# Layer norm in two token halves, statistics on token partitions, a GpSimd power, and the S5 tables spread anew over the first FFN

## The chip, the cores and the metric

The kernel runs on 1 core of one Trainium2 chip. The metric is device time in microseconds, the median of 3 runs. Engine names in the rows: PE is TensorE (PEld its weight loads), DVE is VectorE, ACT is ScalarE, POOL is GpSimd, SP is SyncE. A queue is written SPq or ACTq.

## The reference

Two hybrid decoder layers on 528 tokens (512 and 16 learned meta tokens), model width 1024, float32. Per layer there are three layer norms, after the first FFN, after the gated merge and after the second FFN:

```python
def layer_norm(x, g, b):
    mu = mean(x); var = mean(square(x - mu))
    return (x - mu) * rsqrt(var + LN_EPS) * g + b

x = layer_norm(ALPHA * x + 0.5 * swiglu(x, ...ffn1...), ln1_g, ln1_b)
proj = x @ w_in            # latents, short conv, S5 inputs, gates
y_a, y_b, y_c = attention, short conv, S5 state space model
x = layer_norm(ALPHA * x + (sum of sigmoid(g_i) * y_i) @ w_o, ln2_g, ln2_b)
x = layer_norm(ALPHA * x + 0.5 * swiglu(x, ...ffn2...), ln3_g, ln3_b)
```

`swiglu` is `(silu(x @ w_gate) * (x @ w_up)) @ w_down`, with an inner width of 2816, which is 22 tiles of 128.

## The kernel before

Activations are kept transposed: features on the 128 partitions, the 528 tokens along the free axis, so that x is 8 tiles of 128x528. Each float32 matrix product is made of three fast products in the fp32r format: every operand is split into a high part (`x_hi`, `w_hi`) and a rest (`x_lo`, `w_lo`), and `product` runs hi*hi, lo*hi and hi*lo. A product tile of 528 tokens fills two PSUM banks with 264 tokens each; `pair(k)` is banks 2k and 2k+1 of the 8, `two(x)` is x seen as 2x264. So a weight chunk of 1024 columns costs 8 tiles x 3 products x 2 token halves = 48 matmuls, one of 768 columns 36.

Weights come as 236 chunks for each layer. A chunk `c` goes through four engines. SP loads it into one of two `w_raw` slots once GpSimd has finished with the chunk two before; ACT rounds it to `w_hi` (`round_ahead`, three chunks ahead, as soon as PE is through with the chunk that held the slot); GpSimd makes `w_lo = w_raw - w_hi` (`split`); PE multiplies and counts `chunk_done`. Each engine runs its own list of instructions in order, and the engines meet in semaphores only.

An FFN runs in three parts (`PARTS`, of 8, 8 and 6 inner tiles). In a part, each inner tile needs two chunks (gate and up); ACT applies Silu, and DVE multiplies (L1185) and splits the result (L1186, L1187). Then eight down chunks follow (8 tiles x nf), whose products DVE adds to the residual `z` ("ln_in" in the rows) with one instruction each. While the first FFN runs, DVE also computes the tables of the S5 branch: eight `in_step`s beside the inner tiles of part 0, eight `turn_step`s beside its down chunks, `out_step`s beside part 1.

A norm (`layer_norm` on DVE, `layer_norm_middle` and `layer_norm_end` on PE, `square` and `layer_norm_end` on ACT) works like this. After four of the last eight chunks PE sums the features of z0 to z2 over partitions with a matrix of ones (a 128x128 stationary operand of ones gives the sum in all 128 partitions, L467), and DVE takes this provisional mean away from all tiles. DVE adds up tiles and squares as the other chunks end. PE then sums both over partitions (L467), DVE computes mean and variance for 128x528, ACT takes the root, DVE the reciprocal (L1164). After that each tile passes DVE (scale, L1167), ACT (gain and bias in place, then `x_hi`), and DVE (`x_lo`, L1170), which counts `x_ready`. The next stage begins with `first_products` (L458), which runs three chunks side by side, tile by tile, as `x_ready` counts up. Before the change, the products of all last chunks and of `first_products` write both token halves of a tile.

## Time and profile before

| what | value |
|---|---|
| median of 3 runs | 2853.81 us (2849.2 to 2854.4) |
| the profiled execution, its own time | 2849.89 us |
| its span, first to last instruction | 2848.1 us |
| PE busy | 2680.8 us, 94% |
| DVE / ACT / POOL busy | 1403.8 / 845.6 / 1052.7 us |
| granted TensorE clock, mean | 0.976 of full |

Busy is the share of the span in which an engine has an instruction in work. The profiled execution lies 3.9 us below the median.

### The profile page before, as it was taken

To read this page: it belongs to the slowest core of one execution; us is meant where nothing else is said; L and a number is where in the kernel's file an instruction comes from. 1 tells how busy PE (TensorE), PEld (TensorE's weight loads), DVE (VectorE), ACT (ScalarE), POOL (GpSimd) and SP (SyncE) were. 2 spreads that over 40 slices of the span, in tenths; PEclk is the share of its full clock that TensorE was granted. 3 is DMA by queue.
4 is the path that set the end of the run, shared out by engine and by line. 5 is a ranking of instruction groups with operands and counts; after the bars stand their busy time and mean duration, and the time that the engine had idled before them with its cause. 6 is when DMAs were issued, how large, how long until landed. Compare 5 with 4: busy or idle time off the path is not lost.

```text
span 2848.1 us, 56824 instructions
## 1 busy us (share of the span) xinstructions
PE 2680.8 (94%) x22244; PEld 2601.3 (91%) x22244; DVE 1403.8 (49%) x2020; ACT 845.6 (30%) x1236; POOL 1052.7 (37%) x477
## 2 busy tenths in 40 slices
PE   7999988999999989999789999799999998999996
PEld 7999988988889989999789999799888998999995
DVE  6955154954443652121688641648545337522127
ACT  3222223225522242222242212232345222422123
POOL 3444433322244434444234444233122443344431
PEclk9999999999999999999899999999999999999998
DMA  4323323212223323332223332232122332233322
GB/s 144 96 82 93 89 78 83 71 33 59 55 79 92 97 67 89 89 92 85 69 87 89 89 89 85 71 90 68 40 50 67 78 92 82 82 89 89 89 81 75
DMA packets 458208, 229.30 MB, mean 81 GB/s; under 512 B 38112, under 2 KB 455136, under 8 KB 458048
## 3 DMA queue, kind: packets, MB, share of 16 engines
q1 hardware_dynamic: 452864, 219.98, 27.8%
q10 hardware_dynamic: 5184, 7.14, 0.9%
q8 instruction: 106, 1.74, 0.2%
q14 instruction: 54, 0.44, 0.0%
HBM read 222.83 MB, written 2.10 MB: 79 GB/s over the span
## 4 chain that ended last, share of the span: by engine, by line
issue 51%; PE 25%; POOL 21%; DVE 2%; POOLq 1%; ACT 0%; DMA 0%; SPq 0%; DVEq 0%; ACTq 0%
PE ps L442 21%; POOL w_lo L393 21%; PE ps L458 1%; PE ps L742 1%; PE ps L704 1%; PE ps L721 0%; DVE ln_in L1133 0%; PE ps L467 0%; POOLq L392 0%; PE ps L708 0%; DVE stat L1164 0%; DVE stat L1148 0%; DVE ln_in L1117 0%; POOLq L398 0%; DVE stat L1134 0%
## 5 line engine op out<-in xcount | busy, mean ns | idle before, releaser
L393 POOL TENSOR_TENSOR w_lo<-w_raw,w_hi 128x1024 fp32r<-128x1024 f32 (+3 forms) x472 | 1050.0, 2230 | 1748.0 <-ACT w_hi L830 1747.9
L830 ACT ACTIVATE w_hi<-w_raw 128x1024 fp32r<-128x1024 f32 (+3 forms) x475 | 453.8, 959 | 851.6 <-PE ps L442 724.2
L442 PE MATMUL ps<-x_hi,w_hi 128*128 128x264 f32 x4000 | 543.1, 288 | 20.6 <-ACT w_hi L830 8.1
L442 PEld LDWEIGHTS ps<-x_hi,w_hi 128*128 128x128 f32 x4000 | 507.8, 190 | 32.6 <-issue 23.5
L442 PE MATMUL ps<-x_lo,w_hi 128*128 128x264 f32 x4000 | 528.4, 284 | 0.0
L442 PE MATMUL ps<-x_hi,w_lo 128*128 128x264 f32 x4000 | 526.5, 284 | 0.0
L442 PEld LDWEIGHTS ps<-x_lo,w_hi 128*128 128x128 f32 x4000 | 502.9, 189 | 0.0
L442 PEld LDWEIGHTS ps<-x_hi,w_lo 128*128 128x128 f32 x4000 | 501.0, 188 | 0.0
L1185 DVE TENSOR_TENSOR hid_rest<-hid_rest,ps 128x528 f32<-128x528 f32 x88 | 61.9, 704 | 548.5 <-PE ps L442 524.2
L442 PE MATMUL ps<-hid_hi,w_hi 128*128 128x264 f32 x1408 | 195.8, 290 | 15.5 <-DVE ln_in L1117 14.6
L442 PEld LDWEIGHTS ps<-hid_hi,w_hi 128*128 128x128 f32 x1408 | 181.6, 192 | 18.6 <-DVE ln_in L1117 16.1
L442 PE MATMUL ps<-hid_lo,w_hi 128*128 128x264 f32 x1408 | 190.3, 285 | 0.0
L442 PE MATMUL ps<-hid_hi,w_lo 128*128 128x264 f32 x1408 | 188.9, 284 | 0.0
L442 PEld LDWEIGHTS ps<-hid_lo,w_hi 128*128 128x128 f32 x1408 | 179.6, 190 | 0.0
L442 PEld LDWEIGHTS ps<-hid_hi,w_lo 128*128 128x128 f32 x1408 | 178.0, 189 | 0.0
L1198 DVE SCALAR_TENSOR_TENSOR ln_in<-ps,ln_in 128x528 f32<-128x528 f32 x64 | 45.3, 707 | 255.6 <-PE ps L442 254.4
L1187 DVE TENSOR_TENSOR hid_lo<-hid_rest,hid_hi 128x528 fp32r<-128x528 f32 x88 | 152.8, 1736 | 3.1
L830 ACT ACTIVATE hid_rest<-ps 128x528 f32 x88 | 53.8, 611 | 331.7 <-PE ps L442 331.6
L458 PE MATMUL ps<-x_hi,w_hi 128*128 128x264 f32 x288 | 64.6, 308 | 64.5 <-DVE x_lo L1170 45.1
L1522 DVE SCALAR_TENSOR_TENSOR stat<-stat,ps 128x528 f32<-128x528 f32 x32 | 22.5, 705 | 184.5 <-PE ps L442 184.5
L458 PEld LDWEIGHTS ps<-x_hi,w_hi 128*128 128x128 f32 x288 | 49.6, 209 | 67.2 <-DVE x_lo L1170 47.2
L830 ACT ACT_TABLE_LOAD x53 | 68.0, 1283 | 94.4 <-PE ps L442 59.6
(272 smaller groups left out, 2928.3 us busy)
## 6 DMA issues: line engine op xcount, KB each, us to landing
w_raw<-in_ffn_w_gate SPq DMA_DIRECT2D x91, 512.0 KB, 3.8
w_raw<-in_w_in SPq DMA_DIRECT2D x90, 512.0 KB, 3.9
w_raw<-in_ffn_w_up SPq DMA_DIRECT2D x88, 512.0 KB, 3.8
w_raw<-in_ffn_w_down SPq DMA_DIRECT2D x64, 512.0 KB, 3.9
w_raw<-in_ffn_w_down SPq DMA_DIRECT2D x32, 384.0 KB, 3.3
w_raw<-in_w_o SPq DMA_DIRECT2D x16, 512.0 KB, 3.8
w_raw<-in_conv_w_out SPq DMA_DIRECT2D x16, 256.0 KB, 2.8
w_raw<-in_s_w_out SPq DMA_DIRECT2D x16, 256.0 KB, 3.2
```

The costliest lines, as they stand in the source:

```text
L393: pool.tensor_tensor(w_lo[:, s, 0:n], w_raw[:, c % RAW, 0:n], w_hi[:, s, 0:n].bitcast(f32), ALU.subtract).then_inc(w_split, 1)
L442: ins = nc.tensor.matmul(out[0:m, h], w[:, s, cols], x[:, k0 + k, h * HALF:(h + 1) * HALF], start=first and k == 0 and n == 0, stop=last a ...
L458: ins = nc.tensor.matmul(out[:, h], w[:, (c + j) % SLOTS, k * P:(k + 1) * P], x[:, k, h * HALF:(h + 1) * HALF], start=k == 0 and n == 0, s ...
L704: ins = nc.tensor.matmul(ps[:, j % 2, 0:q0 + P], qT[0:QKD, b, q0:q0 + nq], kT[0:QKD, b, 0:q0 + P], start=True, stop=True)
L742: ins = nc.tensor.matmul(ps[64 * b:64 * b + 64, 4 + 2 * b + half, q0 - half * HALF:HALF], vb[0:nk, b, k, :], PT[0:nk, k, q0:(half + 1) * H ...
L830: return nc.scalar.activation(out, in_, f, **kw)
L1185: st.done(tt(two(glf[:, f]), two(glf[:, f]), pair(2 * (f % 2) + 1), MUL))
L1187: tt(gl[:, f], glf[:, f], ghf[:, f], SUB).then_inc(hid_done, 1)
L1198: ins = stt(two(z[:, d]), pair(d % 2), 0.5 / ALPHA, two(z[:, d]), MUL, ADD)
L1522: ins = stt(two(stat[:, 2]), two(stat[:, n % 2]), 1.0, pair(2 * (n % 2) + 1), ADD, MUL)
```

## The change

Tokens 0 to 263 and 264 to 527 become two halves that pass through a norm one after the other. The last four down (or w_o) chunks are multiplied for the first half, all four, and then for the second half, each 128x264 result in a bank of its own (`HALF_BANK`, `last_tiles`). DVE takes each half tile out of PSUM, takes the provisional mean away and adds it to the sums (`take_half`); ACT squares it. The provisional mean is that of z0 and z1, and stays in PSUM. The sums over features are now made with the tokens as output partitions: the stationary operand is 88 tokens of the sums, the moving operand one column of ones, so that the 264 tokens of a half give 88 partitions x 3 columns (`layer_norm_sums`). DVE computes mean and variance on these 88x3 elements with four instructions, GpSimd raises the variance to the power -0.5 (`root`, `norm`), and PE spreads the mean and the root back over 128 partitions and 264 columns with a matmul against the identity (`layer_norm_wide`); DVE reads both from PSUM (`tail`). ACT no longer uses Sqrt in a norm, DVE no reciprocal there.

The next stage's first four chunks are multiplied for the first half of the tokens and then for the second: two chunks tile by tile, the sums of the second half, the third chunk, the spreading of the second half, the fourth chunk, and then all four for the second half. GpSimd's splits of these four chunks stand between its two powers; ACT's roundings of them stand between its norm tiles. Three of DVE's four `take_half`s of the second half stand in the first half's `tail`, behind tiles 0, 3 and 5.

`PARTS` becomes 6, 8 and 8 inner tiles, so that the last down chunks have 48 matmuls instead of 36. In the first FFN the S5 tables move: `s5_parameters` behind the first inner tile, `in_step`s 0 to 4 in part 0 and 5 to 7 in part 1, `turn_step`s 0 to 5 beside part 0's down chunks and 6 and 7 in part 1, `out_step`s 1 to 3 in part 1 and 4 to 7 in part 2; PE's transposes of them (`turn_inputs`) go from part 0's down chunks to part 1's. z is no longer rebuilt from `x_hi` and `x_lo` in the FFNs (it still holds x); before the w_o norm it is rebuilt in the merge loop. ACT's S5 parameter functions come after the Silu of the first inner tile, and the output leaves in 16 transfers instead of 8.

```diff
-PARTS = [(0, 8), (8, 8), (16, 6)]
+PARTS = [(0, 6), (6, 8), (14, 8)]
 PART_AT = [sum(2 * nf + KD for _, nf in PARTS[:n]) for n in range(len(PARTS))]
...
+HALF_BANK = {4: 0, 5: 2, 6: 1, 7: 3}
...
+            for h, t0 in enumerate((N_META, HALF)):
+                t1 = (h + 1) * HALF
+                for k in range(KD):
+                    sp.wait_ge(ln_out, (3 * DEPTH - 1) * 2 * KD + h * KD + k + 1)
+                    sp.dma_start(t["out"][k * P:(k + 1) * P, t0 - N_META:t1 - N_META], z[:, k, t0:t1]).then_inc(out_written, 16)
+            sp.wait_ge(out_written, 32 * KD)
...
+            def root(l, which, h):
+                pool.wait_ge(ln_var, (l * 3 + which) * 2 + (h + 1))
+                pool.tensor_tensor(tok_root[0:TOK, h], tok_root[0:TOK, h],
+                                   minus_half[0:TOK, :].to_broadcast([TOK, TB]), ALU.pow).then_inc(ln_root, 1)
+            def norm(l, which, c0):
+                root(l, which, 0)
+                for n in range(SLOTS):
+                    split(l, c0 + n)
+                root(l, which, 1)
...
+            def first_products(l, c, x0, n):
+                for h in range(2):
+                    for j in range(2):
+                        pe.wait_ge(z_half[1], n * 4 + (4 + 2 * h + j + 1))
+                    by_tiles(l, [pair(0), pair(1)], c, xh, xl, x_ready[h], x0, halves=(h,))
+                    if h == 0:
+                        layer_norm_sums(n, 1)
+                    for j in (2, 3):
+                        rounded(l, c + j)
+                        ins = product(pair(j), c + j, 0, xh, xl, KD, True, True, split=(l, c + j), halves=(h,))
+                        if h == 1:
+                            ins.then_inc(chunk_done, 1)
+                        elif j == 2:
+                            layer_norm_wide(n, 1)
...
+            def layer_norm_first(l, which):
+                n = l * 3 + which
+                pe.wait_ge(ln_sums, n * 3 + 2)
                 sum_over_features(stat[:, 1], pair(2)).then_inc(ln_stat, 1)
...
+            def layer_norm_sums(n, h):
+                pe.wait_ge(ln_sums, n * 3 + (h + 3))
+                for src, bank in ((stat[:, 1], 4 + h), (stat[:, 2], 6 + h)):
+                    for j in range(TB):
+                        t0 = h * HALF + j * TOK
+                        ins = nc.tensor.matmul(ps[0:TOK, bank, SUM_AT + j:SUM_AT + j + 1], src[:, t0:t0 + TOK],
+                                               ones[:, 0:1], start=True, stop=True)
+                    ins.then_inc(ln_stat, 1)
+            def layer_norm_wide(n, h):
+                pe.wait_ge(const_in, 16 * 5)
+                for ready, src, bank in ((ln_mean, tok_mean, 4 + h), (ln_root, tok_root, 6 + h)):
+                    pe.wait_ge(ready, n * 2 + (h + 1))
+                    for j in range(TB):
+                        ins = nc.tensor.matmul(ps[:, bank, j * TOK:(j + 1) * TOK],
+                                               src[0:TOK, h, j:j + 1].to_broadcast([TOK, P]), ident[0:TOK, 0:TOK],
+                                               start=True, stop=True)
+                    ins.then_inc(ln_wide, 1)
+            def last_tiles(l, which, c, hi, lo, nk):
                 n = l * 3 + which
...
+                t0 = takes_at(l, which, (len(PARTS) - 1) * (which != 1))
+                for h in range(2):
+                    for d in range(WHOLE, KD):
+                        if h == 0:
+                            rounded(l, c + d)
+                            pe.wait_ge(z_taken, t0 + (min(d, 5) + 1))
+                        else:
+                            pe.wait_ge(z_half[0], n * 4 + (d - 3))
+                        bank = HALF_BANK[d]
+                        s = (c + d) % SLOTS
+                        for p, (w, x) in enumerate(((w_hi, hi), (w_hi, lo), (w_lo, hi))):
+                            if p == 2 and h == 0:
+                                split_ready(l, c + d)
+                            for k in range(nk):
+                                ins = nc.tensor.matmul(ps[:, bank, 0:HALF], w[:, s, k * P:(k + 1) * P],
+                                                       x[:, k, HALVES[h]], start=p == 0 and k == 0,
+                                                       stop=p == 2 and k == nk - 1)
+                        ins.then_inc(half_done if h == 0 else chunk_done, 1)
+                        if h == 1 and d == WHOLE:
+                            layer_norm_sums(n, 0)
+                        if h == 1 and d == WHOLE + 1:
+                            layer_norm_wide(n, 0)
...
+                act.wait_ge(ln_dev, n * 12 + (k + 1 if h is None else 1 + k + 4 * h))
+                dst = stat[:, 2] if k == 0 else stat[:, 3 + k % 2]
+                ACTV(dst[:, cols], z[:, k, cols], ACT.Square).then_inc(ln_square, 1)
+            def norm_tile(l, which, k, h):
+                n = (l * 3 + which) * 2 + h
+                col = PC_LN + which * 16 + k
+                act.wait_ge(ln_scaled, n * KD + (k + 1))
+                ACTV(z[:, k, HALVES[h]], z[:, k, HALVES[h]], ACT.Identity, scale=par[:, col:col + 1],
+                     bias=par[:, col + 8:col + 9]).then_inc(ln_out, 1)
+                act.wait_ge(ln_out, n * KD + (k + 1))
+                ACTV(xh[:, k, HALVES[h]], z[:, k, HALVES[h]]).then_inc(ln_hi, 1)
+            def layer_norm(l, which, bd):
+                for d in range(WHOLE):
+                    round_ahead(l, bd + d)
+                for k in range(3):
+                    square(l, which, k)
+                round_ahead(l, bd + WHOLE)
+                square(l, which, 3)
+                for k in range(4, KD):
+                    square(l, which, k, 0)
+                square(l, which, 4, 1)
+                round_ahead(l, bd + 5)
                 for k in range(KD):
...
+                    norm_tile(l, which, k, 0)
+                    if k in (1, 4, 6):
+                        square(l, which, {1: 5, 4: 6, 6: 7}[k], 1)
+                        round_ahead(l, bd + {1: 6, 4: 7, 6: 8}[k])
+                for k in range(KD):
+                    norm_tile(l, which, k, 1)
...
+                def take_half(k, h):
+                    if h == 0:
+                        dve.wait_ge(half_done, n * 4 + (k - 3))
+                    else:
+                        dve.wait_ge(chunk_done, done_at(l, bd + k))
+                    cols = HALVES[h]
+                    ins = stt(z[:, k, cols], ps[:, HALF_BANK[k], 0:HALF], scale, z[:, k, cols], MUL, ADD)
+                    follow(ins, z_half[h], n * 4 + (k - 3) + 4 * h)
+                    follow(tt(z[:, k, cols], z[:, k, cols], ps[:, 6 + h, 0:HALF], SUB), ln_dev, n * 12 + (1 + k + 4 * h))
+                    st.done(tt(S[:, cols], S[:, cols], z[:, k, cols], ADD))
+                def add_square(k, cols=every, square=None):
+                    dve.wait_ge(ln_square, n * 12 + square)
+                    return tt(Q[:, cols], Q[:, cols], stat[:, 3 + k % 2, cols], ADD)
                 take(0)
                 take(1)
...
+                tt(S, z[:, 0], z[:, 1], ADD).then_inc(ln_sums, 1)
                 take(2)
...
+                dve.wait_ge(ln_stat, n * 5 + 3)
+                st.done(ts(pair(3), pair(2), 1.0 / (2 * P), None, MUL))
+                st.done(stt(two(S), pair(3), -2.0, two(S), MUL, ADD))
+                for k in range(3):
+                    tt(two(z[:, k]), two(z[:, k]), pair(3), SUB).then_inc(ln_dev, 1)
+                dve.wait_ge(ln_dev, n * 12 + 3)
+                st.done(tt(S, S, z[:, 2], ADD))
+                st.done(add_square(1, square=2))
                 take(3)
...
+                follow(tt(two(z[:, 3]), two(z[:, 3]), pair(3), SUB), ln_dev, n * 12 + 4)
+                st.done(tt(S, S, z[:, 3], ADD))
+                st.done(add_square(2, square=3))
+                for k in range(WHOLE, KD):
+                    if k == WHOLE:
+                        st.done(add_square(3, square=4))
+                    else:
+                        st.done(add_square(k - 1, HALVES[0], k))
+                    take_half(k, 0)
+                add_square(KD - 1, HALVES[0], KD).then_inc(ln_sums, 1)
+                take_half(WHOLE, 1)
+                def tail(h):
+                    cols = HALVES[h]
+                    mean, root = ps[:, 4 + h, 0:HALF], ps[:, 6 + h, 0:HALF]
+                    sums, squares = (ps[0:TOK, b + h, SUM_AT:SUM_AT + TB] for b in (4, 6))
+                    m_, v_, t_ = (v[0:TOK, h] for v in (tok_mean, tok_root, tok_tmp))
+                    dve.wait_ge(ln_stat, n * 5 + (4 + 2 * h))
+                    follow(ts(m_, sums, 1.0 / D_MODEL, None, MUL), ln_mean, n * 2 + (h + 1))
+                    st.done(tt(t_, m_, m_, MUL))
+                    dve.wait_ge(ln_stat, n * 5 + (5 + 2 * h))
+                    st.done(stt(v_, squares, 1.0 / D_MODEL, t_, MUL, SUB))
+                    ts(v_, v_, LN_EPS / ALPHA ** 2, None, ADD).then_inc(ln_var, 1)
+                    dve.wait_ge(ln_wide, n * 4 + (2 * h + 3))
+                    dev = lambda k: tt(z[:, k, cols], z[:, k, cols], mean, SUB)
+                    dev(0)
+                    st.done(dev(1))
+                    dve.wait_ge(ln_wide, n * 4 + (2 * h + 4))
+                    m = n * 2 + h
+                    for k in range(KD + 1):
+                        if k < KD:
+                            tt(z[:, k, cols], z[:, k, cols], root, MUL).then_inc(ln_scaled, 1)
+                        if k + 2 < KD:
+                            st.done(dev(k + 2))
+                        if k:
+                            dve.wait_ge(ln_hi, m * KD + k)
+                            tt(xl[:, k - 1, cols], z[:, k - 1, cols], xhf[:, k - 1, cols], SUB).then_inc(x_ready[h], 1)
+                        if h == 0 and k in (1, 4, 6):
+                            j = {1: 5, 4: 6, 6: 7}[k]
+                            st.done(add_square(j - 1, HALVES[1], j + 4))
+                            take_half(j, 1)
+                        if h == 0 and k == 7:
+                            add_square(KD - 1, HALVES[1], 12).then_inc(ln_sums, 1)
+                tail(0)
+                tail(1)
...
+            def tables_beside(l, part, f, st):
+                if part == 0 and f == 0:
+                    s5_parameters(l, st)
+                    dve.wait_ge(b_in, l * 32 + 32)
+                if part == 0 and f > 0:
+                    in_step(l, f - 1, st)
+                if part == 1:
+                    if f < 3:
+                        in_step(l, f + 5, st)
+                    elif f == 3:
+                        turn_step(l, 6, st)
+                    elif f == 4:
+                        turn_step(l, 7, st)
+                        cmul(st, [bS[:, 0], bS[:, 1]], each(s5cf[:, 0], 32), each(s5cf[:, 1], 32), by_pair(bS[:, 0]),
+                             by_pair(bS[:, 1]), 32)
+                    else:
+                        out_step(l, f - 4, st)
+                if part == 2 and f < 4:
+                    out_step(l, f + 4, st)
```

## Rows read from the trace of the kernel before

**Rows 1.** Waits of PE: who waited for whom (us in all, times, longest)
```profile
PE ps L458 <- DVE x_lo L1170: 45.1, 5, 9.1
PE ps L442 <- DVE ln_in L1198: 3.2, 4, 1.2
```

**Rows 2.** Windows, PE alone, one per norm: length, busy (matmuls), clock
```profile
395.50:458.00 62.50, 46.09 (x311) 0.84 0.20 51
968.70:1030.20 61.50, 48.81 (x359) 0.92 0.18 52
1381.60:1451.90 70.30, 46.65 (x310) 0.83 0.19 59
1810.00:1871.30 61.30, 43.45 (x310) 0.92 0.20 51
2381.90:2444.10 62.20, 49.83 (x359) 0.89 0.16 48
2795.50:2848.10 52.60, 25.07 (x166) 0.75 0.21 70
```

**Rows 3.** Timeline of PE, first norm: start, length, instructions merged, [idle before]
```profile
395.53 1.05 PE L467 MATMUL ps<-stat,ones 128*128 128x264 f32 x4
...
408.39 3.01 PE L442 MATMUL ps<-hid_hi,w_hi 128*128 128x264 f32 x12 [3.08 <-DVE ln_in L1117]
...
457.97 2.10 PE L442 MATMUL ps<-x_hi,w_hi 128*128 128x264 f32 x16
459.91 2.10 PE L442 MATMUL ps<-x_lo,w_hi 128*128 128x264 f32 x16
```

**Rows 4.** Timeline of PE where layer 1 begins
```profile
1451.90 3.89 PE L442 MATMUL ps<-x_hi,w_hi 128*128 128x264 f32 x16 [7.46 <-POOL w_lo L393]
```

**Rows 5.** Timelines of DVE and ACT, and one group by shape: sizes
```profile
48.58 0.41 DVE L1257 TENSOR_TENSOR s_tmp<-s_coef,s_b_own 128x256 f32<-128x256 f32 x1
...
437.91 0.81 ACT L830 ACTIVATE ln_in<-ln_in,par 128x528 f32<-128x528 f32 x1
438.75 0.64 ACT L830 ACTIVATE x_hi<-ln_in 128x528 fp32r<-128x528 f32 x1
...
L830 ACT ACTIVATE s_u<-ps 128x264 f32<-128x264 f32 x16 | 5.3, 390 | 9.4 <-PE ps L458 9.4
```

**Rows 6.** Timeline of PE in the heads: small plain float32 matmuls
```profile
656.52 0.42 PE L721 MATMUL ps<-ident,probs 16*128 16x16 f32 x4
```

**Rows 7.** Timeline of DVE, first norm: reciprocal, two tiles of the new x
```profile
432.28 3.44 DVE L1164 RECIPROCAL stat<-stat 128x528 f32<-128x528 f32 x1
...
438.04 0.71 DVE L1170 TENSOR_TENSOR x_lo<-ln_in,x_hi 128x528 fp32r<-128x528 f32 x1 [0.21 <-ACT x_hi L830]
...
440.02 0.70 DVE L1170 TENSOR_TENSOR x_lo<-ln_in,x_hi 128x528 fp32r<-128x528 f32 x1
```

**Rows 8.** Groups of POOL by shape, the two smallest
```profile
L393 POOL TENSOR_TENSOR w_lo<-w_raw,w_hi 128x256 fp32r<-128x256 f32 x16 | 13.6, 851 | 34.0 <-ACT w_hi L830 34.0
L1623 POOL MEMSET const-float32-0.0<- 128x1 f32 x1 | 0.1, 100 | 0.3 <-issue 0.3
```

**Rows 9.** Lines L1185 and L1187 (ns min/median/max), and a split beside DVE
```profile
L1185 DVE TENSOR_TENSOR hid_rest<-hid_rest,ps x88: 690/704/705, 41.2 to 2778.2; 128x528 f32<-128x528 f32 x88
L1187 DVE TENSOR_TENSOR hid_lo<-hid_rest,hid_hi x88: 707/1470/2896, 42.4 to 2779.4; 128x528 fp32r<-128x528 f32 x88
...
416.40 2.53 POOL L393 TENSOR_TENSOR w_lo<-w_raw,w_hi 128x1024 fp32r<-128x1024 f32 x1 [3.85 <-ACT w_hi L830]
416.59 2.90 DVE L1148 TENSOR_TENSOR stat<-stat 128x528 f32<-128x528 f32 x1
```

**Rows 10.** Timeline at the kernel's end
```profile
2844.94 0.71 DVE L1170 TENSOR_TENSOR x_lo<-ln_in,x_hi 128x528 fp32r<-128x528 f32 x1 [0.68 <-ACT x_hi L830]
```

**Rows 11.** Timeline of PE at the kernel's start
```profile
18.31 0.81 PE L458 MATMUL ps<-x_hi,w_hi 128*128 128x264 f32 x2 [1.43 <-POOL w_lo L393]
...
40.29 2.10 PE L442 MATMUL ps<-x_hi,w_hi 128*128 128x264 f32 x16
```

289 lines of the change are left out of this document (114 added, 175 removed).

## Prediction

> **What bounds the kernel now.** I read the page first: PE is busy for 94% of the span, every other engine half of it or less, and inside the FFNs PE waits for almost nothing. So the question is where its missing time lies. The waits of PE say it: its largest wait is for `x_lo`, five times 9 us [rows 1]. These are the norms. The reader is to see the same hole six times in the windows [rows 2]: each window runs from the provisional sum (after the fourth of the last eight chunks) to the product behind the first three chunks of the next stage; the sixth ends with the kernel.
>
> The price of a hole is its length less the matmuls in it at full pace. Sixteen matmuls take 1.94 us, 0.121 each (the last two rows of [rows 3]). An FFN norm holds 4 x 36 + 3 x 48 = 288, or 34.8 us; a w_o norm 336, or 40.6 us. The losses: 62.5 - 34.8 = 27.7; 61.5 - 40.6 = 20.9; 70.3 - 34.8 = 35.5; 61.3 - 34.8 = 26.5; 62.2 - 40.6 = 21.6. Behind the third comes a run of 16 matmuls in 3.9 instead of 1.9 us [rows 4], 1.9 more: together 134 us. The sixth holds 144 matmuls (17.4 us) in 52.6 us: 35.2 lost. In the timeline of the first norm the reader sees what a loss is made of: PE waits 3 us for DVE among the last chunks (408.4), again before the sums [rows 3], then 9 us for the root, the reciprocal and the first tile [rows 1].
>
> **A norm after the change, step by step.** Half a tile of a down chunk is 24 matmuls, 2.9 us. T = 0 is where PE starts the first half of chunk 4 of the last eight. I lay out each engine's list in order.
>
> Sizes: a DVE operation on 128x256 takes 0.41 us, and on 264 columns I take 0.43. ACT takes 0.39 for a 128x264 copy; gain and bias on 528 columns is 0.17 longer than `x_hi` (0.81, 0.64), so 0.62 and 0.43 for the half [rows 5]. These are estimates from the rows. One `take_half` with its `add_square` is four DVE operations that wait for each other: 1.8 us.
>
> First halves, T = 0 to 11.6. DVE needs 1.8 us of each 2.9. It starts at 5.7, behind the third tile, three sums and a split that holds one of them, has caught up when the fourth half arrives, and its sums are ready at 13.7. PE sums at 14.5, after chunk 4's second half. Small plain float32 matmuls are two instructions each; four instructions of 16x16 stand in 0.42 us [rows 6], so 0.1 apiece, so that a set of six matmuls (12 instructions) is 1.2 us. Four sets per norm: 4.8 us, and 0.9 for the provisional sum, one matmul set of the kind that takes 1.05 us with its end [rows 3]. DVE's four 88x3 operations end at 16.7.
>
> GpSimd's power has no row. From below it costs 0.1 (its MEMSET on 128x1); from above I take the 0.85 of 128x256 subtracted, times the 5 by which DVE's reciprocal (3.44 us [rows 7]) exceeds its plain operation of that size (0.70), about 4. I take 1.0, since 3 columns are nearest to the MEMSET's one [rows 8]. PE spreads mean and root after chunk 5, at 18.6, so the first power is hidden up to 1.9 us; the second is on the path. At 4 us each it would cost 5 us per norm, 30 in all: that is an end of the range.
>
> `tail` for the first half begins at 20.4. Before, a tile passed every 1.98 us (438.04 to 440.02) [rows 7]. A half tile is three DVE operations in 1.15 us and two on ACT in 1.1. Three tiles carry a `take_half`, 1.8 us, and on ACT a square and a rounding, 1.5 us. And the splits now run beside the tiles: before, the roundings they wait for stood behind ACT's last tile. An operation with one operand in PSUM is never held (690 to 705 ns over 88); one with both in SBUF is held until the split ends (707 to 2896 ns, one stands beside its split) [rows 9]. The subtractions and products of `tail` read PSUM and pass, `x_lo` and the sums don't. Laid out in order, `x_lo` is ready at 22.5, 25.5, 28.3, 29.6, 32.6, 35.4, 37.9 and 41.2: three of the four splits hold an `x_lo` for about 1.5 us.
>
> PE has ended the last chunk at 26.0. The two first chunks need 5.8 us, but are fed until 41.2 and end at 41.95: 10.1 us lost. Then the sums (43.2), the third chunk (46.1), the spreading with the power just in time (47.7), the fourth chunk (50.6). The second half's tiles come from 50.1 every 1.25 us, with no splits among them, so PE ends them at 59.6: 3.2 us lost. Then 5.8 us of work, to 65.4. Work of 384 matmuls is 46.5. Loss: 65.4 - 46.5 + 0.9 = 19.8.
>
> The clock: after a wait of 3.1 us the first 12 matmuls took 3.0 instead of 1.6 us [rows 3]. Feeding in bursts should bring that once or twice. I add 2.0: **21.8 per norm**, five times 109.
>
> TensorE's small matmuls are where a page would price otherwise. The Trainium skill, TensorE: Matmul & The Clock Gate, section "Wait — 56ns, not 53.3ns?", has starts no closer than about 25 ns however few the columns. By it the 48 instructions of a norm would take 1.2 us (estimate from that page), and the change would be worth some 20 us more; the rows of the heads, four times slower, decide here, since each instruction also loads weights.
>
> The sum. Five norms: 109 - 134 = -25. The last norm: the same list, the second sums already at 38.4, the statistics done at 43.8, last tile out of ACT at 53, last transfer 2.5 us behind (2845.65 to 2848.1) [rows 10]: 55.4 + 0.9 - 23.2 = 33.1 lost, against 35.2: -2. The start: two chunks instead of three must be split before PE runs through, so from 18.3 [rows 11]; with 23.2 us of work, 2.4 for an empty sum and spreading and 1.4 of slow clock the fourth chunk ends at 45.3, against 40.3 + 5.8 = 46.1: -1.
>
> The S5 tables. With eight in_steps beside eight inner tiles of 11.6 us (96 matmuls) PE's wait for what DVE takes between parts is 3.2 us over all four FFNs [rows 1]. The new places hold no more work per tile, and z's rebuilding (0.7 per tile) is gone. Tighter are the down chunks of part 0, 36 matmuls or 4.35 us instead of 5.8: the largest step there, six operations on 128x256, is 2.5 us, with the take of 0.7 and a split in between 5.7. The two bank pairs take the overrun up. All at nothing, hidden behind PE's products; with the cover gone it would be 1 or 2 us. But ACT's parameter functions, with their table loads, now stand between two roundings of a running stage: round chunk 4 at 4.9 after the halves end, the functions wait for DVE behind the first inner tile, and chunk 5 is ready about 1 us after PE wants it: +1 per layer, +2. The stall of 7.5 us that the same functions cause at the second layer's start [rows 4] is in the third window above, so it is not counted again. Longer last chunks (`PARTS`) cost nothing, they move matmuls from part 0.
>
> -25 - 2 - 1 + 2 = -26. From the profiled execution's own 2849.9 us that gives 2824; the runs' median lies 3.9 above it, so I predict **2827**.
>
> **Rivals.**
> *Hidden after all.* If PSUM reads and the split times fall luckily (no `x_lo` held, 4.5 us; one clock fall less, 1), a norm loses 16.3: five 82, total -53, 2800. For it: the powers and sums of the first half lie behind products. Against: in the first `tail` DVE alone has 14.6 us of work (8 x 1.15 + 3 x 1.8), where PE has 11.6.
> *The splits take it all.* GpSimd's four splits of 2.5 us could each hold DVE for their whole length, 10 us instead of 4.5, so 5.5 more per norm: +27, 2855, no change. The row shows the full hold of 2.2 us [rows 9]. The Trainium skill, SBUF — State Buffer, section "Who interferes with whom", has it as a rule: the port is locked for a whole instruction, and whoever issued first keeps it. By that rule four splits under a chain of DVE operations are a risk; the trace agrees.
> *Slower: the step doesn't halve.* The chain DVE, ACT, ACT, DVE with its semaphores may set the pace of a tile, so that a half tile takes near the 1.98 us of a whole one. Then the first `tail` is 7 x 0.8 = 5.8 longer and the second as much: 11.6 per norm, +58, 2885. It decides from 1.15 up to 1.15 + 5.2 / 14 = 1.5 us per half tile; above that the change loses. For it: fixed costs don't shrink, and there are twice as many hand-overs. Against: DVE's halves take 0.41 of 0.70, and the software order has two tiles in flight. A power of 4 us goes the same way, to 2855.
> *The clock stays low.* Bursts of 0.7 us each 2.5 us could keep TensorE at 1.2 GHz through all of the next four chunks. Against: at 408.4 it was back at full pace behind 12 matmuls [rows 3], and each of the new chunks has 24 in a row. Three falls of 1.4 to 1.8 us instead of one: 3 us more per norm, 2842. The Trainium skill, TensorE: Matmul & The Clock Gate, section "HAM oscillation — how this bites in real kernels", warns of just such work between waits.
>
> **How the numbers follow.** Forecast 0.50, between 2808 and 2845; hidden after all 0.22; splits take it all 0.10; slower 0.13; clock 0.05. The range leaves out the luckiest tenth and the slowest tenth: 2785 to 2862. A difference under 0.2% (5.7 us) this measurement can't tell from none. Faster: nearly all of the first two and the clock's, 0.76; same 0.09; slower 0.15.
>
> **What would show it.** In each norm: `x_lo` of the first half every 1.2 us with gaps where `take_half` stands, each of 1.8; PE waiting about 10 us in pieces before L458's successor, then some 3 us in the second half; DVE operations with two SBUF operands at up to 2.9 us beside splits, those from PSUM at 0.43; 12 small matmul instructions in 1.2 us; the power near 1 us; no long wait before chunk 5 of an FFN; the last tile's `x_hi` 53 us after T. Wrong would be: a power of several us, a half tile slower than 1.5 us, or PE fed so early that the first halves end at 32.

## The result, and the profile after

The changed kernel takes 2819.0 us (median of 4 runs, 2817.1 to 2822.2), the kernel before 2852.4 beside it: a ratio of 0.9885, 95% interval 0.9868 to 0.9902. The forecast was 2827. The profiled execution has a span of 2816.6 us against 2848.1, so 31.5 less, where the sum said 26.

First the waits of PE, all those of 1.2 us in sum or more but the ones inside the mixers, as the view groups them (total, times, longest). They answer to [rows 1].

```profile
PE ps L489 <- DVE x_lo L1289: 34.8, 41, 2.2
PE ps L489 <- POOL w_lo L408: 22.4, 6, 12.6
PE ps L528 <- DVE stat L1238: 12.1, 1, 12.1
PE ps L473 <- ACT w_hi L915: 7.0, 3, 3.8
...
PE ps L473 <- DVE hid_lo L1310: 2.9, 1, 2.9
...
PE ps L473 <- DVE ln_in L1317: 1.2, 2, 0.7
```

One wait of 9 us per norm for the first `x_lo` has become eight or so short ones. Then the windows of PE, one per norm, as in [rows 2] (length, busy and matmuls, granted clock, DMA). They begin at the provisional sum, which now stands a chunk earlier, and end with the fourth chunk of the next stage, one later than before: 432 matmuls, 52.2 us at full pace.

```profile
386.39:459.45 73.06, 65.16 (x486) 0.91 0.20 51
957.91:1031.82 73.91, 65.79 (x486) 0.91 0.18 53
1362.59:1435.66 73.07, 64.41 (x486) 0.93 0.22 63
1779.22:1852.20 72.98, 65.24 (x486) 0.91 0.20 52
2350.06:2424.21 74.15, 65.65 (x487) 0.91 0.18 53
2754.97:2816.60 61.63, 37.51 (x294) 0.80 0.25 76
```

The losses are 20.9, 21.7, 20.9, 20.8 and 22.0, together 106 us; 109 was forecast, and 134 stood before (with 1.9 behind the third window; 1.8 stand there now, and N3 in the table below has both). The last loses 32.6 (forecast 33.1). The first norm on PE's timeline, T = 0 at 393.10; it can be laid beside the forecast's list:

```profile
407.64 1.03 PE L528 MATMUL ps<-ones,stat 128*88 128x1 f32 x12
...
411.53 0.80 PE L538 MATMUL ps<-ident,token_mean 88*128 88x88 f32 x6
...
425.50 0.39 PE L489 MATMUL ps<-x_hi,w_hi 128*128 128x264 f32 x1 [1.89 <-DVE x_lo L1289]
...
428.01 0.59 PE L489 MATMUL ps<-x_hi,w_hi 128*128 128x264 f32 x1 [1.46 <-DVE x_lo L1289]
...
434.99 1.82 PE L528 MATMUL ps<-ones,stat 128*88 128x1 f32 x12
...
441.16 0.80 PE L538 MATMUL ps<-ident,token_mean 88*128 88x88 f32 x6
```

Sums at T = 14.5 (forecast 14.5), spread at 18.4 (18.6), the first halves' tiles done at 41.9 (41.95), the whole at 66.4 (65.4). The same twelve small instructions took 1.03 us in the first of these rows and 1.82 in the fifth, because the granted clock had fallen in between, while PE worked in bursts of 0.7 us between waits of 1 to 2 us. It was back for the second half (windows of PE, the clock is the last but two):

```profile
393.10:426.20 33.10, 29.67 (x247) 1.00 0.21 54
426.20:440.00 13.80, 10.22 (x48) 0.51 0.28 77
440.00:459.45 19.45, 18.55 (x143) 1.00 0.02 5
```

GpSimd's new group by shape, beside the smallest split's (busy and mean ns, idle before):

```profile
L408 POOL TENSOR_TENSOR w_lo<-w_raw,w_hi 128x256 fp32r<-128x256 f32 x16 | 13.6, 848 | 34.4 <-ACT w_hi L915 34.4
L424 POOL TENSOR_TENSOR token_root<-token_root,minus_half 88x3 f32<-88x3 f32 x12 | 10.2, 847 | 102.1 <-DVE token_root L1275 102.1
```

And the timelines of VectorE and GpSimd in the first norm:

```profile
425.01 0.43 DVE L1289 TENSOR_TENSOR x_lo<-ln_in,x_hi 128x264 fp32r<-128x264 f32 x1
...
426.01 1.95 DVE L1289 TENSOR_TENSOR x_lo<-ln_in,x_hi 128x264 fp32r<-128x264 f32 x1 [0.23 <-ACT x_hi L915]
...
425.10 2.57 POOL L408 TENSOR_TENSOR w_lo<-w_raw,w_hi 128x1024 fp32r<-128x1024 f32 x1 [4.37 <-ACT w_hi L915]
```

The power takes 0.85 us, and a split from 425.10 to 427.67 holds an `x_lo` that needs 0.43 until 427.96. So inside a norm nearly every row stands where it was forecast. The stretches outside don't. At the start of the first FFNs PE now waits for ScalarE:

```profile
66.86 3.01 PE L473 MATMUL ps<-x_hi,w_hi 128*128 128x264 f32 x16 [3.80 <-ACT w_hi L915]
...
1437.60 2.19 PE L473 MATMUL ps<-x_hi,w_hi 128*128 128x264 f32 x16 [1.77 <-ACT w_hi L915]
...
1445.08 2.17 PE L473 MATMUL ps<-x_hi,w_hi 128*128 128x264 f32 x16 [1.42 <-ACT w_hi L915]
```

while the second FFN has no wait left at all. In layer 1 these are the fifth and sixth chunks, whose roundings stand around the parameter functions. In layer 0 it is the eighth, and the rounding that it waits for had itself waited for a load:

```profile
65.69 1.06 ACT L915 ACTIVATE w_hi<-w_raw 128x1024 fp32r<-128x1024 f32 x1 [1.71 <-DMA w_raw<-in_ffn_w_gate]
```

A chunk is loaded into one of two slots when an earlier split has ended, so a rounding held up by the parameter functions (it stands at 47.43, behind them) makes a split late and with it the next load. That is read off the timelines; that the order is the cause, e7 tests. And before, the loss behind `w_o`, where the last tiles had 48 matmuls already, was 21, what it is now; only the norms behind an FFN gained. The following table is the frame for the experiments. Each number is what PE lost in a stretch of the profiled execution: its length less its matmuls at 0.1208 us each (16 in 1.933). N1 to N6 are the norms in order (N2 and N5 behind `w_o`; N3 up to the fifth chunk of layer 1, with the waits ahead of it); A1, A2 the first FFNs of the layers between the norms' windows, B1, B2 the second.

| kernel | N1 | N2 | N3 | N4 | N5 | N6 | A1 | B1 | A2 | B2 | span |
|---|---|---|---|---|---|---|---|---|---|---|---|
| before | 27.7 | 20.9 | 37.5 | 26.5 | 21.6 | 35.2 | 7.2 | 3.4 | 8.2 | 3.4 | 2848.1 |
| after | 20.9 | 21.7 | 22.8 | 20.8 | 22.0 | 32.6 | 10.3 | 0.2 | 11.0 | 0.2 | 2816.6 |
| e1 after, boundary wait back | 20.8 | 21.8 | 23.1 | 20.8 | 21.8 | 32.6 | 12.9 | 3.4 | 14.3 | 3.4 | 2825.6 |
| e2 before, boundary wait moved | 27.6 | 19.7 | 36.0 | 27.8 | 19.7 | 34.4 | 4.2 | 0.1 | 5.1 | 0.2 | 2827.2 |
| e3 before, parts 8, 6, 8 | 19.9 | 21.6 | 32.0 | 22.6 | 21.6 | 30.2 | 8.3 | 3.4 | 8.4 | 3.4 | 2825.9 |
| e4 after, parts 8, 8, 6 | 27.8 | 21.9 | 28.2 | 27.6 | 21.8 | 37.9 | 9.3 | 0.1 | 9.3 | 0.1 | 2837.6 |
| e5 before, both edits | 21.2 | 21.5 | 29.3 | 21.4 | 21.5 | 30.2 | 6.1 | 0.2 | 6.2 | 0.2 | 2813.8 |
| e6 e5, fourth chunk first | 19.9 | 21.0 | 22.1 | 21.4 | 21.5 | 30.2 | 5.3 | 0.2 | 15.0 | 0.2 | 2809.1 |
| e7 after, parameters later | 21.6 | 22.0 | 21.0 | 22.0 | 21.7 | 32.6 | 5.0 | 0.2 | 10.4 | 0.2 | 2810.3 |
| e8 after, spreads earlier | 21.1 | 21.1 | 22.1 | 21.1 | 20.7 | 32.6 | 10.1 | 0.2 | 12.3 | 0.2 | 2816.5 |
| e9 e6, parameters later | 19.9 | 21.4 | 20.0 | 21.2 | 21.5 | 30.2 | 15.6 | 0.2 | 13.9 | 0.2 | 2817.3 |
| e10 after, narrow splits | 13.8 | 16.6 | 15.8 | 16.6 | 18.0 | 28.9 | 11.3 | 0.2 | 10.8 | 0.2 | 2783.0 |
| e11 after, power thrice | 22.6 | 22.2 | 24.4 | 22.1 | 22.0 | 34.8 | 10.1 | 0.2 | 13.9 | 0.2 | 2830.5 |
| e12 e5, narrow splits | 16.2 | 15.4 | 22.7 | 15.8 | 16.6 | 30.1 | 5.3 | 0.2 | 7.6 | 0.2 | 2788.0 |

The start and the mixers make up the rest. The mixers' code is the same in all, and what their stretch in the second layer lost by the same count still varied from 123.5 to 129.2 us (e10 and e9 against e12), so a single span says nothing about less than some 5 us. Single norms are steadier: N2, which has the same code in before, e2, e3, e5, e6 and e9, lost 19.7 to 21.6. The ratios of the timed runs, each to the kernel before on its own chip, stand with each experiment.

### The profile page after: what moved, and what is told of

It reads as the page before. It is cut to its first block, busy times and chain, and to the rows that moved or that the text cites. A ratio compares the mean times of both kernels' runs of the same rounds, so it can differ in the third digit from the quotient of the medians.

```text
span 2816.6 us, 58024 instructions
## 1 busy us (share of the span) xinstructions
PE 2699.4 (96%) x22460; PEld 2619.6 (93%) x22460; DVE 1371.3 (49%) x2257; ACT 844.3 (30%) x1333; POOL 1069.1 (38%) x492
## 4 chain that ended last, share of the span: by engine, by line
issue 50%; PE 26%; POOL 22%; DVE 1%; POOLq 1%; ACT 1%; DMA 0%; SPq 0%; DVEq 0%; ACTq 0%
POOL w_lo L408 22%; PE ps L473 21%; PE ps L560 1%; PE ps L824 1%; PE ps L786 1%; PE ps L489 1%; PE ps L803 0%; DVE ln_in L1277 0%; DMA w_raw<-in_ffn_w_gate 0%; POOLq L407 0%; PE ps L790 0%; DVE ln_in L1284 0%; ACT w_hi L915 0%; PE ps L538 0%; DVE x_lo L1289 0%
## 5 line engine op out<-in xcount | busy, mean ns | idle before, releaser
L915 ACT ACTIVATE w_hi<-w_raw 128x1024 fp32r<-128x1024 f32 (+2 forms) x476 | 457.2, 964 | 844.4 <-PE ps L473 711.6
L473 PE MATMUL ps<-x_hi,w_hi 128*128 128x264 f32 x4096 | 561.7, 289 | 12.6 <-ACT w_hi L915 7.0
L915 ACT ACTIVATE hid_rest<-ps 128x528 f32 (+1 forms) x88 | 53.8, 611 | 366.3 <-PE ps L473 351.8
L473 PE MATMUL ps<-hid_hi,w_hi 128*128 128x264 f32 x1152 | 157.9, 286 | 1.2 <-DVE ln_in L1317 1.2
L473 PE MATMUL ps<-hid_hi,w_lo 128*128 128x264 f32 x1152 | 155.1, 284 | 0.0
L473 PE MATMUL ps<-hid_lo,w_hi 128*128 128x264 f32 x1152 | 155.0, 283 | 0.0
L473 PEld LDWEIGHTS ps<-hid_hi,w_hi 128*128 128x128 f32 x1152 | 146.0, 188 | 2.6 <-DVE ln_in L1317 1.6
L473 PEld LDWEIGHTS ps<-hid_hi,w_lo 128*128 128x128 f32 x1152 | 145.7, 188 | 0.0
L473 PEld LDWEIGHTS ps<-hid_lo,w_hi 128*128 128x128 f32 x1152 | 145.6, 188 | 0.0
L489 PE MATMUL ps<-x_hi,w_hi 128*128 128x264 f32 x192 | 66.3, 346 | 57.2 <-DVE x_lo L1289 34.8
L1661 DVE SCALAR_TENSOR_TENSOR stat<-stat,ps 128x528 f32<-128x528 f32 x32 | 22.6, 705 | 176.0 <-PE ps L473 176.0
L915 ACT ACTIVATE ln_in<-ln_in,par 128x264 f32<-128x264 f32 x96 | 57.6, 600 | 99.1 <-DVE ln_in L1284 98.9
```

Of the source, the lines that this page charges most:

```text
L473: ins = nc.tensor.matmul(out[0:m, h], w[:, s, cols], x[:, k0 + k, HALVES[h]], start=first and k == 0 and n == 0, stop=last and k == n_tile ...
L489: ins = nc.tensor.matmul(out[:, h], w[:, (c + j) % SLOTS, k * P:(k + 1) * P], x[:, k, HALVES[h]], start=k == 0 and n == 0, stop=k == KD - ...
L915: return nc.scalar.activation(out, in_, f, **kw)
L1661: ins = stt(two(stat[:, 2]), two(stat[:, n % 2]), 1.0, pair(2 * (n % 2) + 1), ADD, MUL)
```

## The experiments

**e1 and e2: one wait at the part boundaries.** The diff moves a line that the forecast passed over. Before, PE waited at the start of each FFN part for VectorE's take of the last down tile (`t0 + 2`). Now it waits there for the one before it, and for the last only ahead of the first up chunk, whose banks it frees. e1 undoes this in the changed kernel, e2 does it in the kernel before.

```diff
# e1, in the changed kernel
-                        pe.wait_ge(z_taken, t0 + 1)
+                        pe.wait_ge(z_taken, t0 + 2)
# e2, in the kernel before
-                    pe.wait_ge(z_taken, t0 + 2)
+                    pe.wait_ge(z_taken, t0 + (2 if part == 0 else 1))
...
                             rounded(l, c + 1, i * 4)
+                            pe.wait_ge(z_taken, t0 + 2)
```

> The changed kernel with one line as it was before: TensorE waits at the start of the second and third part of each FFN for VectorE's take of the last down tile, not of the one before it. Theory A (that take is late at each of the eight part boundaries; before, six waits of 1.35 us sum to 8.1 though the view puts them down to w_hi, and after none is there in the second FFN): 9 to 10 us slower than the changed kernel, 2828 to 2829, ratio to the kernel before 0.9915, with one wait of about 1.35 us at each boundary. Rival B (those waits are really for ScalarE's rounding, cured by the longer lead elsewhere): the same as the changed kernel, 2819.

> The kernel before with that one wait moved alone: at a part boundary TensorE waits for the take of the last but one down tile, and for the last one's only ahead of the first up chunk. Theory A: 8 to 10 us faster than before, 2843 (ratio 0.997), the six waits for w_hi of 8.1 us in the chain of TensorE's waits gone. Rival B: no change, 2852.

e1: 2831.2 us, ratio 0.9938 (0.9924 to 0.9951), against 0.9885 without the edit. e2: 2834.5 us, ratio 0.9945 (0.9932 to 0.9958), some 16 us faster than before. Theory A holds, and its price was too low: 3.0 to 3.3 us per FFN in e2 (A and B columns), 12.6 in all, as it takes 12.3 in e1. (The norms, the mixers and the start account for the rest of e2's span, 4.2, 3.2 and 0.9 us less; the edit doesn't touch them.) The view had put six of the eight waits down to the wrong engine. The boundary on PE's timeline in e1, then ScalarE and VectorE at that time, then the changed kernel's PE and ScalarE at the same boundary:

```profile
2512.90 1.83 PE L473 MATMUL ps<-x_hi,w_hi 128*128 128x264 f32 x13 [1.34 <-ACT w_hi L915]
...
2511.74 1.06 ACT L915 ACTIVATE w_hi<-w_raw 128x1024 fp32r<-128x1024 f32 x1 [3.30 <-PE ps L473]
...
2511.59 0.71 DVE L1317 SCALAR_TENSOR_TENSOR ln_in<-ps,ln_in 128x528 f32<-128x528 f32 x1 [3.64 <-PE ps L473]
```

```profile
2505.60 2.09 PE L473 MATMUL ps<-x_hi,w_hi 128*128 128x264 f32 x16
...
2505.95 1.06 ACT L915 ACTIVATE w_hi<-w_raw 128x1024 fp32r<-128x1024 f32 x1 [3.30 <-PE ps L473]
```

In e1 a rounding ends 0.1 us before PE starts, so it looks like the releaser. In the changed kernel PE starts 0.35 us before that same rounding begins: PE never needed it. The take ends at 2512.30; why PE needs 0.6 us more (its loop's set-up behind the wait would be one reason) was not tried.

**e3 and e4: the length of the last tiles.** `PARTS` moves two inner tiles from the first part to the last, so the tiles ahead of an FFN's norm have 48 matmuls, not 36. The forecast had that cost nothing and gain nothing. e3 does it alone, e4 undoes it (in both, table steps follow so that none is lost).

```diff
# e3, in the kernel before
-PARTS = [(0, 8), (8, 8), (16, 6)]
+PARTS = [(0, 8), (8, 6), (14, 8)]
# e4, in the changed kernel
-PARTS = [(0, 6), (6, 8), (14, 8)]
+PARTS = [(0, 8), (8, 8), (16, 6)]
```

> The kernel before with the FFN parts cut 8, 6, 8 in place of 8, 8, 6, so that the last down tiles are of 48 matmuls, not 36 (the tables follow). The matmuls are as many. Theory P (the norms behind an FFN lost 27 us and those behind w_o 21 only because their last tiles were shorter; both lose 21 after the change): 6 us less at each of three norms and 3 at the end, about 20 us faster, 2832. Rival H (it is the two halves that gain, the tiles' length does nothing): 2852. Between them the share of each can be read.

> The changed kernel with the FFN parts cut 8, 8, 6 as before: halves, statistics on tokens and power kept, last tiles of 36 matmuls. Theory P: the norms behind an FFN lose 6 us more again, 2837 to 2840. Rival H: 2819 to 2822.

e3: 2828.6 us, ratio 0.9923 (0.9908 to 0.9937), 22 us faster than before. e4: 2840.8 us, ratio 0.9967 (0.9955 to 0.9980), 23 us slower than the changed kernel by the ratios. Theory P holds both ways: N1, N4 and N6 go from 27.7, 26.5 and 35.2 to 19.9, 22.6 and 30.2 in e3, and from 20.9, 20.8 and 32.6 to 27.8, 27.6 and 37.9 in e4. So at N1 and N4 the halves with tiles of 36 lose what whole tiles of 36 lost before, and at N6 2.7 more. What the tile length does is on PE's timeline, first norm, of e5 (below), to be laid beside [rows 3] and beside this row of before, the wait for the sums:

```profile
423.27 3.89 PE L467 MATMUL ps<-stat,ones 128*128 128x264 f32 x8 [3.90 <-DVE stat L1148]
```

The rows of e5:

```profile
402.00 2.20 PE L442 MATMUL ps<-hid_hi,w_hi 128*128 128x264 f32 x16 [0.84 <-DVE ln_in L1118]
...
408.37 2.20 PE L442 MATMUL ps<-hid_hi,w_hi 128*128 128x264 f32 x16 [0.31 <-DVE ln_in L1118]
...
416.90 2.05 PE L467 MATMUL ps<-stat,ones 128*128 128x264 f32 x8 [2.46 <-DVE stat L1149]
...
429.83 0.81 PE L458 MATMUL ps<-x_hi,w_hi 128*128 128x264 f32 x2 [9.10 <-DVE x_lo L1171]
```

VectorE's rounds from one take to the next are as long in both kernels, 8.4, 6.4 and 7.1 us before and 8.3, 6.4 and 7.1 in e5. They outlast PE's tile of 4.35 us by far, its tile of 5.8 us by less. The 3.08 us ahead of 408.39 in [rows 3] are 0.84 here, and the wait for the sums 2.46 (3.90 before). The clock is part of the price: behind the longer waits the first twelve matmuls took 3.0 us and the eight of the sums 3.89, against 2.05 for these eight in e5. The 9.1 us for the first `x_lo` are untouched, and yet the loss is 21.

**e5 and e6: the kernel before with both edits, and with ScalarE's order too.** e5 is e2 and e3 together: whole-tile norms, no halves, no power. e6 adds this:

```diff
# e6, on top of e5; the first two f's are taken out of ScalarE's loop
                 st = Steps(act, act_step, l, ACT_STEPS)
+                round_ahead(l, B_FFN1)
                 act.wait_ge(x_ready, l * 24 + 8)
```

> The kernel before with the boundary wait moved (as in the run of it alone, which gave 3.2 us at each of four FFNs) and the parts cut 8, 6, 8 (which gave 8 us at the first norm, 4 and 2 at the third and fourth, 5 at the end); whole-tile layer norms, statistics and square root as before, no power on GpSimd. Theory P (the changed kernel's gain is these two, and the halves add nothing): 2848 - 13 - 19 to 21 = 2814 to 2817, ratio 0.987 to 0.988, so no slower than the changed kernel. Rival H (the gains overlap, and the halves carry the rest): 2825 or more.

> The run before this one, and ScalarE rounds the fourth chunk of a layer ahead of the wait for x_ready, its five DMA issues and the parameter functions, which are now behind it. Theory: the wait of 7.5 us for that chunk's w_lo at the second layer's start goes, with the slow clock behind it, 8 to 10 us less than the kernel with both edits, 2805 to 2808, faster than the changed kernel by 11 to 14. Rival: the x_lo that the chunk's products then wait for takes it over, and less than 3 us are gained.

e5: 2817.2 us, ratio 0.9893 (0.9878 to 0.9908). That is the changed kernel's 0.9885 within both intervals: **two edits of a few lines give the whole gain, and the halves give none of it.** In the table e5's norms lose 145.1 us in sum and the changed kernel's 140.8; all of the difference and more is N3 (29.3 against 22.8), the wait of 7.7 us for the fourth chunk's `w_lo`, and that is ScalarE's order again. The four norms with neither that wait nor the kernel's end in them, N1, N2, N4 and N5, lose 85.6 us in e5 and 85.4 in the changed kernel; at N6 the halves lose 2.4 more.

Why the halves gain nothing can be read off the first norm. In e5 PE waits 12.7 us (0.84, 0.31, 2.46 and 9.10), and its sums over features take 4.5. In the changed kernel no wait is longer than 2 us, but the two stretches that are fed tile by tile lose 10.5 and 2.4 us, 12.9 together, and the small sums and spreads take 5.8. The rest is mostly the lower clock: 3.0 us in e5's products behind its long wait, 1.5 in the changed kernel's third chunk. The wait was cut into pieces, not shortened.

e6: 2815.9 us, ratio 0.9888 (0.9872 to 0.9904). N3 gives its 7.2 us, as expected, but A2 takes 8.8 back: the rival's outcome, though with another row than it named. PE's one long wait in that FFN:

```profile
1443.17 3.86 PE L442 MATMUL ps<-x_hi,w_hi 128*128 128x264 f32 x16 [6.97 <-DVE hid_lo L1198]
```

The reading was that VectorE stands at its parameters ahead of the first inner tile, so that a PE that comes earlier only waits later.

**e7 and e9: the parameters later.** e7 puts ScalarE's five parameter DMA issues and its parameter functions behind the second Silu, and moves VectorE's table steps one inner tile on. e9 does it on top of e6.

```diff
# e7, ScalarE of the changed kernel
                 gate(0, 0, 0, ahead=False)
+                gate(0, 0, 1)
                 if w == 0:
+                    parameter_loads(l)
                     act.wait_ge(s5p_in, l * 16 + 16)
...
-                gate(0, 0, 1)
# e7, VectorE
-                if part == 0 and f == 0:
+                if part == 0 and f == 1:
                     s5_parameters(l, st)
# e9, VectorE's in-steps j by inner tile f
+                            for j in {2: (0,), 3: (1,), 4: (2,), 5: (3,), 6: (4, 5), 7: (6, 7)}.get(f, ()):
```

> The changed kernel with ScalarE's parameter DMA issues and parameter functions behind the second Silu of a layer's first FFN, and VectorE's table steps one f later. Theory: TensorE's waits of 3.8 + 3.2 us for w_hi and 2.9 us for hid_lo at the start of the first FFNs (losses there 10.3 and 11.0 us against 4.2 and 5.1 with the boundary wait alone moved) shrink by 8 to 10 us in all, 2809 to 2811. Rival: the parameters come late for VectorE, which then holds up hid_lo of the next f for as long, 2819 or more.

> The kernel before with the boundary wait moved, parts 8, 6, 8, ScalarE's fourth chunk first (the three of the last such run), and now the parameter DMA issues and functions behind the second Silu as well, VectorE's parameters behind the second f and its in-steps behind f = 2 to 7. The last such run saved 7 us at the third norm and gave 9 back in the second layer's first FFN (a wait of 7.0 us for hid_lo). Theory: that wait was VectorE standing at its parameters ahead of the first f; both gains hold, the first FFN of the second layer loses 5 to 6 us and the third norm 22, 2800 to 2806, ratio 0.984 to 0.986. Rival: the longer run of parameters between two f holds hid_lo up elsewhere, no faster than 2813.

e7: 2812.7 us, ratio 0.9876 (0.9860 to 0.9893), the fastest kernel here that computes everything. A1 goes from 10.3 to 5.0, N3 from 22.8 to 21.0, and no wait for `w_hi` is left; A2 changes little (11.0 to 10.4), since waits for `hid_lo` of 1.1 and 3.2 us come in. By the medians that is 6 us less than the changed kernel, by the ratios 3, of 8 to 10 expected; it was measured on another chip and the intervals of the ratio overlap: likely, not proven. Since e7 moves ScalarE's functions and VectorE's steps together, it doesn't tell the two apart. e9 fell: 2825.8 us, ratio 0.9929 (0.9915 to 0.9943). The wait of 6.97 us is gone, so its reading was right, and N3 is at 20.0, but A2 loses 13.9 all the same (15.0 in e6) and A1 rose to 15.6:

```profile
127.20 0.81 PE L442 MATMUL ps<-hid_hi,w_hi 128*128 128x264 f32 x2 [6.02 <-DVE hid_lo L1197]
```

That is the end of the first part, where two table steps had been packed behind one inner tile. VectorE had no room for them ahead of the `hid_lo` that the down chunks need; the same wait costs 4.3 us in layer 1.

**e8: the spreads earlier.**

```diff
# in last_tiles, and likewise between the passes of the third chunk
+                            if p == 2 and h == 1 and d == WHOLE + 1:
+                                layer_norm_wide(n, 0, (0,))
```

> The changed kernel with TensorE's spreads back moved ahead: the first half's mean in the middle of the sixth tile's second half, its root right behind that tile; the second half's mean and root between the three passes of the third chunk. Theory: VectorE's idle 2.2 us before its first dev and 4.8 us before the second half's shrink to about 1 and 2, x_lo comes that much earlier, and each norm with a next FFN loses 1 to 3 us less, 2804 to 2814. Rival: the splits on GpSimd and ScalarE's round trip hold x_lo and not the spread, within 2 us of 2819.

2820.0 us, ratio 0.9906 (0.9889 to 0.9921): no gain, as the rival had it. PE's waits for `x_lo` fell from 34.8 to 29.3 us, yet the first five norms lose 106.1 in place of 108.2, and A1 and A2 together 22.4 in place of 21.3. So the spreads were not what set the pace. Whether the splits did, as the rival says, is for e10 to show.

**e11: the power three times.**

```diff
+                for m in range(2):
+                    pool.tensor_tensor(tok_junk[0:TOK, which * 4 + h * 2 + m], tok_root[0:TOK, h],
+                                       minus_half[0:TOK, :].to_broadcast([TOK, TB]), ALU.pow)
```

> The changed kernel with two more powers of the same 88x3 values, into a tile that nobody reads, ahead of each real one on GpSimd (0.85 us each, 1.7 us more). Theory: the first half's power ends 0.45 us ahead of the tile that TensorE does meanwhile, so 1.25 us of the 1.7 show at each of six norms, and the second half's is hidden for 3 us behind the third chunk: 7 us slower, 2826. Rival: the power was not on the path, 2819; or both are fully on it, 2838.

2829.1 us, ratio 0.9934 (0.9919 to 0.9950), about 14 us more than the changed kernel by the ratios; the norms give 7.3 of it (140.8 to 148.1), and 2.9 stand in A2, which the theory doesn't explain. The wait is there by name, in seven places: 0.44 us in the first half of each norm, and 1.59 in the second half of the last, where no chunk covers it:

```profile
PE ps L542 <- POOL token_root L428: 4.2, 7, 1.6
```

That the norms come to the theory's 7 us is in part luck, since it expected 1.25 us to show in each first half. In the changed kernel no wait of PE is for the power. In the first norm it ends at 411.08, and PE starts to spread the root at 412.17: hidden, with 1.1 us to spare, not the 0.45 of the theory, which had the spread of the mean in mind.

**e10 and e12: what the splits cost.** Four splits of GpSimd run inside each norm. e10 cuts them to 128 of 1024 columns in the changed kernel. e12 does the same in e5, for the first four chunks behind each norm, and for the launch's first four as well. Both leave out the rest of that `w_lo`. The edit of e10:

```diff
                 for n in range(SLOTS):
-                    split(l, c0 + n)
+                    split(l, c0 + n, cols=P)
```

> The changed kernel with GpSimd's four splits inside each norm cut to 128 of their 1024 columns (the rest of that w_lo is left out). Theory: a split holds VectorE's x_lo (1.72 to 1.95 us against 0.43, three times in the first half) and nothing else costs as much there, so the first half's waits for x_lo shrink by 2 to 4 us a norm, 2800 to 2810. Rival: ScalarE's two passes and round trip set the pace of x_lo with or without the splits, 1 us a norm or less, 2813 to 2819.

> The kernel before with the boundary wait moved and parts 8, 6, 8, and the first four splits behind each layer norm cut to 128 of their columns (the rest of that w_lo is left out, and set to zero once at the start); those of the launch's first chunks are cut as well, so the start is read apart. Its partner is the changed kernel with the same cut, whose norms lost 13.8 to 18.0 us in place of 20.8 to 22.0. Theory: whole-tile norms (19.9 to 23.1 us with full splits, 29.3 where the wait of 7.7 us stands) have the splits beside their longest wait, 9 us for the first x_lo, too, but gain less, 1 to 3 us a norm, so that the halves are worth 3 us a norm or more once the splits are out of the way: norms at 18 to 20, whole 2800 to 2810. Rival: the splits cost whole tiles as much, norms at 14 to 17, 2785 to 2795, and the halves are worth nothing in either case.

e10: 2787.6 us, ratio 0.9805 (0.9781 to 0.9829). e12: 2788.1 us, ratio 0.9777 (0.9760 to 0.9794). In e10 the six norms lose 31.1 us less, 5 each; the group of `x_lo` on VectorE shows the hold itself, in the changed kernel and in e10:

```profile
L1289 DVE TENSOR_TENSOR x_lo<-ln_in,x_hi 128x264 fp32r<-128x264 f32 x96 | 66.1, 688 | 19.3 <-ACT x_hi L915 11.8
```

```profile
L1289 DVE TENSOR_TENSOR x_lo<-ln_in,x_hi 128x264 fp32r<-128x264 f32 x96 | 41.5, 432 | 19.3 <-ACT x_hi L915 11.8
```

24.6 us of VectorE's time go, 4.1 per norm, three holds of 1.3 to 1.5. The first norm's window then has the full clock, 1.00 in place of 0.91:

```profile
386.76:452.78 66.02, 60.73 (x487) 1.00 0.22 57
```

In e5 a good part of the hold was elsewhere, in the additions of squares, and goes as well (e5, then e12; 11.0 us in all):

```profile
L1149 DVE TENSOR_TENSOR stat<-stat 128x528 f32<-128x528 f32 x24 | 27.9, 1163 | 0.8
```

```profile
L1154 DVE TENSOR_TENSOR stat<-stat 128x528 f32<-128x528 f32 x24 | 16.9, 704 | 0.8
```

Here my theory fell. Whole tiles gain as much: their norms lose 28.3 us less, and N1, N2, N4 and N5 lose 16.2, 15.4, 15.8 and 16.6 (mean 16.0), the halves 13.8, 16.6, 16.6 and 18.0 (16.3). With the splits or without, the halves are worth nothing.

## Why the prediction was right, and where it was wrong

The time was in its range, and 8 us from the point; faster, as forecast. But the mechanism was wrong. The gain was credited to the halves and belongs to the tile length (the step that failed), and a changed wait was left out (-12.6 us) while a term at +2 came to about +12. These last two nearly cancel, and that is luck.

- **The norm after the change** was right, row by row: 21.8 forecast, 20.8 to 22.0 measured; in the first norm three of four splits hold an `x_lo` for 1.3 to 1.5 us; the second half's tiles come every 1.24 us (1.25); the power is 0.85 us and hidden (1.0); twelve small instructions take 0.9 us at the full clock and 1.7 at the lower (1.2).
- **"Longer last chunks (`PARTS`) cost nothing, they move matmuls from part 0": failed.** True of cost, but the difference between 27 and 21 us in [rows 2] was just that. The text worked both losses out, had the reason for the larger in view (3.08 us for VectorE at 408.39), and put the fall to 21.8 down to the halves. By e3, e4 and e5 tile length is worth 4 to 8 us at each of N1, N3, N4 and N6, and the halves nothing measurable at N1, N2, N4 and N5. The sum didn't suffer, since it counted the norms after the change with tiles of 48 matmuls.
- **"PE's wait for what DVE takes between parts is 3.2 us" [rows 1]: failed.** It was 12.6 us with what goes with it. Two of the eight boundaries are in the 3.2 (1.1 us each); the other six stood in the same view under ScalarE's `w_hi`, 8.1 us, unlisted, and the diff's moved wait wasn't costed at all. "Inside the FFNs PE waits for almost nothing" was the sentence that closed the matter too soon.
- **ScalarE's parameter functions, "+1 per layer, +2", mis-sized:** from e2 to the changed kernel A1 and A2 rise by 6.1 and 5.9 us, 1.9 and 1.1 of them already in e5, with the moved inner tiles. The text had one chunk, the sixth, ready 1 us late. In layer 0 it was the eighth chunk, 3.8 us late; in layer 1 the fifth, sixth and one `hid_lo` by 1.8 (counted in N3), 1.4 and 2.9 us. e7 takes 5.3 of A1 and 1.8 of N3 away by order alone.
- **The S5 tables at nothing:** not separable from the line above; A1 in e7, with the same steps, is 5.0, next to 4.2 in e2.
- **The last norm** -2.6 (-2) and **the start** -0.6 (-1) came as forecast, the first by luck: -5.0 by the longer tiles (e5) and +2.4 by the halves; the wait of 7.46 us [rows 4] went, as the third window said, and is in e5 still there.
- **The rivals:** "The step doesn't halve" is out (1.24 us a half tile), and so is "Hidden after all", since `x_lo` was held. "The clock stays low" is out in the first norm: one fall, for 13.8 us, in which the sums and the third chunk lost 2.4 us beside the waits; the forecast had 2.0. "The splits take it all" is half true: they cost about 5 us a norm, clock and all, but cost the whole tiles as much. The Trainium skill, SBUF — State Buffer, section "Who interferes with whom", says that the port is locked for a whole instruction. The trace agrees: the `x_lo` begun at 426.01 under a split from 425.10 ended 0.29 us behind it.

So the span's -31.5 divides, by the table: -12.6 for the boundary wait (e2); -24.3 for the longer tiles (all norms, before to e5; 4.2 of it stand in e2 too, where no tile is longer, so 20 to 24); -6.5 for the fourth chunk's order at N3 (e5 to after); +2.2 for the halves with their power (the other five norms, e5 to after, all of it at N6); +12.1 for the parameters, the table steps and the moved inner tiles together (e2 to after, all four FFNs); -0.6 at the start and -1.6 in the mixers. Each part is good to a few us, since so much moves between executions of the same code.
